# The high and the low part of a split weight, side by side in one tensor

## What is computed

```python
for l in range(DEPTH):
    n = rms_norm(h, mix_norm_g[l])
    proj = jnp.einsum("btd,de->bte", n, w_in[l])
    ...
    h = h + jnp.einsum("btd,de->bte", merged, w_out[l])
    f = rms_norm(h, ffn_norm_g[l])
    a = jax.nn.silu(jnp.einsum("btd,df->btf", f, w_ffn_gate[l])) * jnp.einsum("btd,df->btf", f, w_ffn_up[l])
    h = h + jnp.einsum("btf,fd->btd", a, w_ffn_down[l])
...
h = h + 0.5 * swiglu(rms_norm_2(h, ffn1_norm[i]), ffn1_w_gate[i], ffn1_w_up[i], ffn1_w_down[i])
```

## Time and profile before

| | |
|---|---|
| median of 3 runs | 3560.92 us (3560.88 to 3561.52) |
| the profiled execution | 3565.33 us |
| its span, from first to last instruction | 3563.4 us |
| granted TensorE clock, mean over the span | 0.987 of full speed |
| TensorE busy | 3435.1 us |
| VectorE busy | 2382.9 us |
| pool engine busy | 2042.8 us |
| ScalarE busy | 993.5 us |

### The profile page before, as it was taken

One profiled execution on the slowest core, in us unless ns is written; L12 is line 12 of the kernel. 1 busy time (PEld: TensorE's weight loads), 2 busy tenths in 40 slices (PEclk: granted clock), 3 DMA queues, 4 the chain that ended last, 5 costly groups with the idle time before them and its releaser, 6 DMA issues.

```text
span 3563.4 us, 49689 instructions
## 1 busy us (share of the span) xinstructions
PE 3435.1 (96%) x19988; PEld 2982.4 (84%) x19988; DVE 2382.9 (67%) x3005; ACT 993.5 (28%) x1716; POOL 2042.8 (57%) x1100
## 2 busy tenths in 40 slices
PE   7999899999999999999999999999999999999997
PEld 7899789999999879977778778878887875788886
DVE  6787898877833578888888863386336765743435
ACT  4406442312110241654232110111114444322201
POOL 4355334655766645533566766677665662466674
PEclk9999999999999999999999999999999999999998
DMA  3122111222323322211223432343335441223332
GB/s 137 60 89 78 48 48 66 83 89 96 126 89 100 111 68 89 81 55 56 83 86 106 147 127 101 100 147 127 100 104 203 142 154 52 91 94 100 101 106 71
DMA packets 96898, 348.29 MB, mean 98 GB/s; under 512 B 10848, under 2 KB 13152, under 8 KB 93664
## 3 DMA queue, kind: packets, MB, share of 16 engines
q1 hardware_dynamic: 80064, 289.44, 24.7%
q10 hardware_dynamic: 16672, 56.70, 4.2%
HBM read 322.32 MB, written 23.79 MB: 97 GB/s over the span
## 4 chain that ended last, share of the span: by engine, by line
PE 75%; DVE 18%; ACT 3%; issue 2%; DMA 1%; POOL 0%; ACTq 0%; DVEq 0%; POOLq 0%
PE acc L521 23%; PE acc L522 22%; PE acc L524 22%; DVE cu L2088 3%; PE acc L783 1%; PE aux L835 1%; DVE ptmp L2291 1%; PE acc L864 1%; PE aux L710 1%; DVE pap L2291 1%; DVE fpr L1821 1%; DVE mtmp L1875 1%; DVE pcp L2291 1%; PE aux L690 1%; PE aux L754 1%
## 5 line engine op out<-in xcount | busy, mean ns | idle before, releaser
L494 POOL TENSOR_SCALAR whi<-raw 128x1024 fp32r<-128x1024 f32 x548 | 624.9, 1140 | 1447.0 <-PE acc L524 1425.9
L496 POOL TENSOR_TENSOR wlo<-raw,whi 128x1024 fp32r<-128x1024 f32 x548 | 1418.0, 2588 | 45.7
L521 PE MATMUL acc<-nhi_s,whi 128*128 128x512 f32 x1568 | 619.8, 395 | 19.6 <-DVE fpr L1818 6.1
L524 PE MATMUL acc<-nhi_s,wlo 128*128 128x512 f32 x1568 | 612.0, 390 | 0.0
L522 PE MATMUL acc<-nlo_s,whi 128*128 128x512 f32 x1568 | 612.0, 390 | 0.0
L521 PE MATMUL acc<-bhi,whi 128*128 128x264 f32 (+1 forms) x1864 | 555.9, 314 | 12.3 <-ACT tqg L1149 5.5
L522 PE MATMUL acc<-blo,whi 128*128 128x264 f32 (+1 forms) x1864 | 542.0, 307 | 0.0
L524 PE MATMUL acc<-bhi,wlo 128*128 128x264 f32 (+1 forms) x1864 | 447.0, 306 | 0.0
L521 PEld LDWEIGHTS acc<-bhi,whi 128*128 128x128 f32 x1864 | 354.1, 190 | 43.4 <-issue 10.5
L521 PEld LDWEIGHTS acc<-nhi_s,whi 128*128 128x128 f32 x1568 | 295.3, 188 | 92.7 <-issue 13.5
L522 PEld LDWEIGHTS acc<-blo,whi 128*128 128x128 f32 x1864 | 353.8, 190 | 14.9
(11 more groups left out here) (410 smaller groups left out, 5865.1 us busy)
## 6 DMA issues: line engine op xcount, KB each, us to landing
raw<-in_w SPq DMA_DIRECT2D x548, 512.0 KB, 3.3
kept_cp<-pcp ACTq DMA_DIRECT2D x4, 1280.0 KB, 6.4
cp<-kept_cp ACTq DMA_DIRECT2D x4, 1280.0 KB, 10.2
kept_ap<-pap ACTq DMA_DIRECT2D x4, 1024.0 KB, 6.1
kept_cs<-pcs ACTq DMA_DIRECT2D x4, 1024.0 KB, 6.4
ap__151<-kept_ap ACTq DMA_DIRECT2D x4, 1024.0 KB, 6.9
cs__162<-kept_cs ACTq DMA_DIRECT2D x4, 1024.0 KB, 6.8
merge_gates<-gout ACTq DMA_DIRECT2D x16, 256.0 KB, 2.2
```

The costliest lines, as they stand in the source:

```text
L494: pool.tensor_scalar(hi, w, 1.0, 0.0, ALU.mult, ALU.add).then_inc(sem("w_hi"), 1)
L496: pool.tensor_tensor(lo, w, hi.bitcast(F32), ALU.subtract).then_inc(sem("w_split"), 1)
L521: pe.matmul(acc[s][:, f, 0:TH], hi, xh[:, f * TH:(f + 1) * TH], start=a, stop=False)
L524: m = pe.matmul(acc[s][:, f, 0:TH], lo, xh[:, f * TH:(f + 1) * TH], start=False, stop=z)
```

## The change

The two tensors `whi` and `wlo`, each with the 1024 elements of a slot in a row, become one tensor `wparts` with a last dimension of two. `whi` is its element 0 and `wlo` its element 1. The names go on being used in the same places, but as views in which neighbouring elements are 8 bytes apart. The high part of a weight is followed by its low part. The total size is the same.

```diff
-        whi = fixed("whi", [P, 2, BLK * P], F32R)
-        wlo = fixed("wlo", [P, 2, BLK * P], F32R)
+        wparts = fixed("wparts", [P, 2, BLK * P, 2], F32R)
+        whi, wlo = wparts[:, :, :, 0], wparts[:, :, :, 1]
```

## The result

The changed kernel takes 3617.76 us (median of 4 runs, 3617.02 to 3621.54) where the kernel before took 3561.22 us on the same chip: a ratio of 1.0157, 95% interval 1.014 to 1.0175. It is 56.5 us slower. The forecast was no change at all.

A forecast was written before the change was run, and what follows sets the result against it. TensorE, busy for 3435.1 of 3563.4 us, was taken to bound the kernel, with splits hidden. Profiled 3565.3 + 0 for loads and pool instructions - 4.4 to the median = 3561 us; range 3549 to 3754.

The forecast's parts named there:

- rival 1: Pool engine's writes get dearer, first instruction 1.0 us longer; TensorE waits 21 us, VectorE adds 30: 3612 us, chance 0.19.
- Bound, slack of the splits: Pool engine's two-instruction weight splits are hidden behind TensorE, which waited for them only 8 times, 3.5 us in all.
- Weight loads: TensorE's loads at lines 521, 522, 524: up to 9 ns more each is free, each further ns costs 9.6 us; taken zero.
- Pool instructions: The pool engine's two instructions per split: bounded by 3.3 us more in all, taken as zero.
- the table of the prediction: TensorE's waiting if every split lengthens by e: 0.25, 0.5, 1, 1.5, 2, 3.3 us give 3, 7, 21, 69, 193, 741 us.
- 59 splits: Splits where VectorE sets the pace, from its 640 us of the chain; half of each added us reaches VectorE, 30 us.
- Rival 2: TensorE's weight loads at half pace, 226 ns apart; 9600 matmuls of 264 columns wait 104 ns each: 4559 us, chance 0.14.
- The estimate by bytes: TensorE's loads at 8 bytes a column span 9.1 bytes per ns, like the streamed operand's 9.0, so no cost.
- Rival 3: Second pool instruction 0.3 us shorter from reading and writing neighbouring words: 3549 us, chance 0.07.
- The last sentence of the prediction: What would make it wrong: 8 bytes as dear as ScalarE's 16, or loads 10 to 30 ns longer, costing 10 to 200 us.

The follow-up runs named there:

- reading alone: Against the kernel before, only TensorE's weight loads step by 8 bytes; the pool engine writes both parts contiguously: 3601.26 us, ratio 1.0108.
- halves: Weight loads step by 8 bytes for the low weights only or the high only, pool engine contiguous, against the kernel before: 3581.36 us and 3597.83 us.
- writing alone: Against the kernel before, only the pool engine's accesses to the two weight parts step by 8 bytes; TensorE loads contiguously: 3579.25 us, ratio 1.0047.

## Why the prediction was right or wrong

The time lies inside the range, 3549 to 3754, and close to rival 1's 3612. Neither is a success: the forecast was 3561, and rival 1's mechanism makes 17 of the 56 us.

- **Bound, slack of the splits: right.** The splits stayed hidden: TensorE's waits for them are 2.0 us in the trace of after, 4 times, against the 3.5 us of the earlier trace rows.
- **Weight loads: the step that failed.** "Against 122.3 ns for a 264-column matmul that leaves 9 ns; against 226.7 ns for a 512-column one, 113 ns. [...] So up to 9 ns a load costs nothing". The length of a load was forecast well: 6 ns more, within the 9. What failed is the premise that a load which is shorter than the matmul beside it costs that matmul nothing. The 512-column matmuls, which I had put aside as safe, pay 6.7 ns each: of the group that reads `nhi_s` there are 3 x 1568 and of the one that reads `ahi_s` 3 x 528 in the trace, the two largest groups, 6288 x 6.7 = 42 us, against 39 measured with reading alone. The 264-column ones, which I had watched, pay nothing, except the 1056 on `ahi` and `alo`, at 121.2 ns in the trace before, which go to 5.18 / 42 = 123.3 (2 us in all).
- **What took its place.** By the places that its allocations give them, the kernel before had the 512-column activations with rows of 2048 bytes (`nhi_s`, `ahi_s`, `ghi_s`, `mhi` and their low parts) at distances of a multiple of 512 bytes from the weights, and that is a favourable position: 226.7 ns a matmul. Moving the activations by 256 or 512 bytes keeps it, by 64 costs 2.3 ns in most blocks (5.44 to 5.49 or 5.50 us) and 6.7 in nine, and moving the weights by 32 costs the whole 6.7; a step of 8 bytes in the loads costs the whole too, with the activations shifted by 64 bytes or not. That contiguous loads of unchanged length give the same 5.60 us, that halves don't add, and that shift and step don't add, is shown. That a step costs what it does because of the same thing as a shift is argued from the equal size. That load and stream meet in some part of SBUF that the low bits of the address choose fits most of this, and is argued too: no run looked at the memory itself, shifts of 8, 16 or 128 bytes were not tried, and it doesn't say why blocks with equal addresses run at two paces (5.49 and 5.60 us with the shift of 64, 5.60 and 5.65 with reading alone). A pace that also depends on what ran just before is the rival that is left, and no run tests it.
- **A row of the trace before said so, and I didn't read it.** The blocks on `bhi` with 512 columns start 64 bytes into rows of 2112 bytes; those of `mg_att1`, one of which is shown, stand between blocks on `nhi_s`. Kernel before, then after, pool timeline:

```profile
1735.05 1.05 POOL L494 TENSOR_SCALAR whi<-raw 128x1024 fp32r<-128x1024 f32 x1 [1.92 <-PE acc L524]
...
1740.63 1.05 POOL L494 TENSOR_SCALAR whi<-raw 128x1024 fp32r<-128x1024 f32 x1 [1.73 <-PE acc L524]
```

```profile
1744.92 1.13 POOL L494 TENSOR_SCALAR wparts<-raw 128x1024 fp32r<-128x1024 f32 x1 [1.96 <-PE acc L524]
...
1750.49 1.13 POOL L494 TENSOR_SCALAR wparts<-raw 128x1024 fp32r<-128x1024 f32 x1 [1.61 <-PE acc L524]
```

  5.58 us with contiguous loads, where the same 24 matmuls on `nhi_s` take 5.44, and 5.57 after. The rows of `bhi` move on by 64 bytes against the weights from piece to piece, so six of the eight pieces are off the favourable distance already; that they had little to lose fits this. In nine such blocks of the trace before the fourth and the eighth piece, at a multiple of 256 bytes, are the quickest, 690 ns for three matmuls against 695 to 714 for the others, but they don't reach the 680 of `nhi_s`. The same matmul at two paces, in one trace, was the sign that the pace depends on something other than columns. The 264-column blocks read rows of 2112 bytes as well, the second half of each from 1056 bytes on, which may be why they hardly change; that was not tried.
- **Pool instructions: nearly right in size, wrong in reach.** Zero was taken; they cost 0.07 and 0.04 us. By the table of the prediction (e of 0.25 us gives 3 us) that hides from TensorE, as it did. (The table comes out of the trace if about 0.1 us is kept between the end of a split and the next one's start.) I had charged VectorE only where it sets the pace all the time, 59 splits, by a half. It pays far more widely: with writing alone 44 us of its busy time for 64 us of the pool engine's, and 12 us of the span show it, 17 by the medians.
- **Rival 2: wrong at 8 bytes, right at 16 for the 264-column matmuls.** It put the doubling of a load at the wrong step. The estimate by bytes, that a step of 8 is only half of what ScalarE's dear rows have, held for the load.
- **Rival 3** found no support: `L496` got longer, not shorter.
- The last sentence of the prediction thought of a load 10 to 30 ns longer. It named a cost without another row changed; the row that changed is the block distance with 512 columns.

The rule of the Trainium skill's "Vector Engine (DVE) Microarchitecture Reference", section 5.2, is about VectorE's ports. Taken over to TensorE and the pool engine, as the prediction tried, it would have brought rivals 1 and 2; the runs show 5% on a load and 7% on the pool engine's first instruction. The rule of the Trainium skill's "GPSIMD Engine Reference", section 7, is about reads; for a write with a step of 8 bytes the runs show 1.13 us where the contiguous one takes 1.06.

No version here beats the kernel before: the one that lies closest to the change, high and low in alternating runs of 128 words, ties with it.

## What to carry to other kernels

A change of layout does two things: it changes the steps of the accesses, and it changes where streams that run at the same time lie relative to each other. Price both; being shorter than the work beside it hides how long an access takes, but not that it may slow that work. When one shape of matmul runs at two paces in one trace, compare how far its weights and its activations lie apart before taking the faster pace for granted. And ask of an engine that gets slower whose instructions get longer beside it, not only who waits for its result.

## What the runs showed of the hardware

- Moving contiguous weights, and what lies behind them, by 32 bytes costs 0.5% of this kernel: 226.7 to 233.3 ns for a 512-column matmul whose activations stayed, nothing for one whose activations moved along. 64 bytes of the activations cost 0.3%, 256 and 512 nothing.
- Bare loads of 128 columns of 4 bytes start 112 ns apart when contiguous, and 118, 173 and 234 ns apart with steps of 8, 12 and 16 bytes.
- With a step in the loads of line 524 alone, 264-column blocks got faster, 5.87 to 5.83 us (121 of 129 such distances are 5.82 or 5.83), and 5.8 us less in sum. With the weights 32 bytes up about half of them take 5.84 or 5.85. With steps in the high weights' loads alone they take 5.86 to 5.88. Why is open.
- In the trace of reading alone 52 blocks take 5.65 us and not 5.60, 50 of them in one run of blocks at `up3` and `down3`. This was not tied to a cause.
